# Finishing an encoder layer inside its expert stage: the last stage's tiles handled behind experts 8 to 11, rows rewritten behind 12 to 14

## The reference

```
aff = jax.nn.softmax((xf @ w_router).astype(jnp.float32), axis=-1)
cap = EC_CAPACITY_FACTOR * n // N_EXPERTS          # 2 * 1024 // 16 = 128
gate, idx = lax.top_k(aff.T, cap)                  # each expert picks 128 tokens
xe = xf[idx]
hid = jax.nn.silu(jnp.einsum('ecd,edf->ecf', xe, w_gate)) * jnp.einsum('ecd,edf->ecf', xe, w_up)
ye = jnp.einsum('ecf,efd->ecd', hid, w_down) * gate[..., None].astype(h.dtype)
y = jnp.zeros_like(xf).at[idx.reshape(-1)].add(ye.reshape(-1, D))
...
x = x + gate2 * rmsnorm(expert_choice_moe(h, ...), g_post_ffn)
```

## Time and profile before

| | us |
|---|---|
| median of 3 runs | 2588.22 |
| the profiled execution's own time | 2585.97 |
| its span in the profile | 2584.2 |
| PE busy | 2305.1 (89%) |
| DVE busy | 1200.7 (46%) |
| ACT busy | 1090.8 (42%) |
| POOL busy | 620.2 (24%) |

### The profile page before, as it was taken

How to read it: one execution, slowest core, us unless ns; L and a number is a source line. 1 busy time by engine, 2 the same in 40 slices (tenths; PEclk the granted TensorE clock), 3 DMA queues, 4 the chain that set the end, 5 groups by cost and what they waited for, 6 DMA issues and landing times. The chain is left out here.

```text
span 2584.2 us, 35356 instructions
## 1 busy us (share of the span) xinstructions
PE 2305.1 (89%) x13449; PEld 1920.3 (74%) x13449; DVE 1200.7 (46%) x1847; ACT 1090.8 (42%) x1758; POOL 620.2 (24%) x615
## 2 busy tenths in 40 slices
PE   6999999999999978999606999999999999999940
PEld 4679889678898876677405888888888888888830
DVE  4212344544224346656493555555555545445416
ACT  4213444645434346655312444444444444444412
POOL 2003234233224234534311011111111111101003
PEclk9999999999999989999758999999999999999975
DMA  8635448456454477645345566666666666666529
GB/s 330 229 98 185 141 149 229 128 160 165 149 174 150 155 189 214 202 146 198 108 192 179 201 207 217 219 212 212 215 218 216 215 220 215 203 204 217 180 55 384
DMA packets 234890, 496.09 MB, mean 192 GB/s; under 512 B 36448, under 2 KB 127600, under 8 KB 231696
## 3 DMA queue, kind: packets, MB, share of 16 engines
q1 hardware_dynamic: 196528, 414.31, 47.6%
q0 software_dynamic: 35936, 71.75, 10.5%
q10 hardware_dynamic: 2304, 8.39, 0.8%
HBM read 405.40 MB, written 88.51 MB: 191 GB/s over the span
## 5 line engine op out<-in xcount | busy, mean ns | idle before, releaser
L2252 DVE TENSOR_TENSOR moe_w_lo<-moe_wf,moe_w_hi 128x2048 fp32r<-128x2048 f32 x192 | 439.9, 2292 | 550.7 <-ACT moe_w_hi L2174 550.7
L2174 ACT ACTIVATE moe_w_hi<-moe_wf 128x2048 fp32r<-128x2048 f32 x192 | 367.9, 1916 | 620.6 <-PE moe_acc L2305 602.1
L2305 PE MATMUL moe_acc<-moe_w_hi,moe_x_hi 128*128 128x512 f32 x1024 | 402.6, 393 | 6.9 <-ACT moe_hid L2188 5.5
L2305 PE MATMUL moe_acc<-moe_w_hi,moe_x_lo 128*128 128x512 f32 x1024 | 399.9, 390 | 0.0
L2305 PE MATMUL moe_acc<-moe_w_lo,moe_x_hi 128*128 128x512 f32 x1024 | 399.4, 390 | 0.0
L2305 PEld LDWEIGHTS moe_acc<-moe_w_hi,moe_x_hi 128*128 128x128 f32 x1024 | 192.9, 188 | 46.8 <-issue 6.0
L1732 PE MATMUL banks<-fr_w_hi,fr_h_hi 128*128 128x256 f32 x768 | 225.5, 294 | 0.0
L2305 PEld LDWEIGHTS moe_acc<-moe_w_hi,moe_x_lo 128*128 128x128 f32 x1024 | 192.8, 188 | 40.6
L2305 PEld LDWEIGHTS moe_acc<-moe_w_lo,moe_x_hi 128*128 128x128 f32 x1024 | 193.0, 189 | 39.3
L1732 PE MATMUL banks<-fr_w_lo,fr_h_hi 128*128 128x256 f32 x768 | 218.2, 284 | 0.0
L1732 PE MATMUL banks<-fr_w_hi,fr_h_lo 128*128 128x256 f32 x768 | 218.0, 284 | 0.0
(11 more groups left out here) (257 smaller groups left out, 4198.3 us busy)
## 6 DMA issues: line engine op xcount, KB each, us to landing
moe_wf<-in_w_expert_gate SPq DMA_DIRECT2D x64, 1024.0 KB, 4.9
moe_wf<-in_w_expert_up SPq DMA_DIRECT2D x64, 1024.0 KB, 4.8
moe_wf<-in_w_expert_down SPq DMA_DIRECT2D x64, 1024.0 KB, 5.1
fr_w_raw<-in_w_units SPq DMA_DIRECT2D x28, 1024.0 KB, 6.0
fr_bias<-in_na_bias SPq DMA_DIRECT2D x16, 1520.0 KB, 11.5
fr_a_w<-in_w_ada POOLq DMA_DIRECT2D x16, 1024.0 KB, 6.3
scratch_qk_t<-fr_stage SPq DMA_DIRECT2D x64, 256.0 KB, 2.5
scratch_vov<-fr_stage SPq DMA_DIRECT2D x96, 128.0 KB, 2.0
```

Source lines behind the costliest of these rows:

```text
L2174: nc.scalar.activation(w_hi[:, q, :, :], wf[:, q, :, :], ACT.Copy).then_inc(w_hi_ready, 1)
L2252: nc.vector.tensor_tensor(w_lo[:, q, :, :], wf[:, q, :, :], w_hi[:, q, :, :].bitcast(F32), ALU.subtract).then_inc(w_lo_ready, 1)
L2305: mm = nc.tensor.matmul(acc[:, j, b, :], x[:, g, k, :], w[:, q, a, h * HALF:(h + 1) * HALF], start=(k == 0 and i == 0), stop=(k == KC - 1 ...
```

## The change

`finish` is gone. Its work is cut into 30 units, done by the engines of `experts` in windows of four behind the experts. Units 0 to 15 are the 16 whole tiles, in windows of the bodies of experts 9 to 12, that is, when the adds of experts 8 to 11 have landed. Units 16 to 29 are the 128 rows that one of experts 9 to 15 picked in one group: their y and x1 are gathered again by index, and the result overwrites these rows of `out`. Sixteen to 19 (experts 9 and 10) stand in the body of expert 13, 20 to 23 in 14's, 24 to 27 in 15's. Units 28 and 29 are the rows of expert 15, whose DOWN product is not weighed and scattered any more: DVE adds it from PSUM, times the gate, to the gathered y (`add_last`). Two buffers each, `fy` and `fx`, serve the units in turn. All their DMAs are issued by POOL: `load_unit`, `root`, `store_unit`. ACT has `square`, DVE `mean`, `result`. For experts 8 to 15 the code is written out, the loop covers 0 to 7.

The diff, without declarations and the body of `finish`:

```diff
+    FIRST, UNITS = 8, 4
+    units = [(t // TT, t, None) for t in range(GROUPS * TT)]
+    units += [(g, None, e) for e in range(FIRST + 1, NE) for g in range(GROUPS)]
...
         def over_experts(eng, body):
-            with eng.Fori(0, NE // 2 - 1) as i:
+            with eng.Fori(0, FIRST // 2) as i:
                 for j in range(2):
                     body(i * 2 + j, j)
-            for j in range(2):
-                body(NE - 2 + j, j)
+            for e in range(FIRST, NE):
+                body(e, e % 2)
+        def window(e):
+            return range(UNITS * (e - FIRST - 1), UNITS * (e - FIRST)) if isinstance(e, int) and e > FIRST else range(0)
...
             def body(e, j):
                 load(e, UP)
+                if isinstance(e, int) and e == FIRST:
+                    for g in range(GROUPS):
+                        sp.dma_start(rows[:, g, :], mod_row[g, GATE2:GATE2 + 1, :].to_broadcast([P, D])).then_inc(rows_loaded, 16)
+                    sp.dma_start(fy[:, 0, :], io["g_post_ffn"].to_broadcast([P, D])).then_inc(rows_loaded, 16)
...
+            def load_unit(n):
+                j = n % 2
+                g, t, e = units[n]
+                if n >= 2:
+                    pool.wait_ge(out_stored[j], 16 * (n // 2))
+                if t is not None:
+                    pool.dma_start(fy[:, j, :], y_view[t]).then_inc(fy_loaded[j], 16)
+                    pool.dma_start(fx[:, j, :], x1_view[t]).then_inc(fx_loaded[j], 16)
+                else:
+                    nc.gpsimd.tensor_copy(row_ids[:, j:j + 1], index_c[:, g * NE + e:g * NE + e + 1])
+                    pool.drain()
+                    at = bass.IndirectOffsetOnAxis(ap=row_ids[:, j:j + 1], axis=0)
+                    pool.indirect_dma_start(fy[:, j, :], None, io["y"], at).then_inc(fy_loaded[j], 16)
+                    pool.indirect_dma_start(fx[:, j, :], None, io["x1"], at).then_inc(fx_loaded[j], 16)
+            def root(n):
+                pool.wait_ge(y_mean, n + 1)
+                nc.gpsimd.tensor_tensor(y_r[:, n % 2:n % 2 + 1], y_ss[:, n % 2:n % 2 + 1], mhalf[:, :], ALU.pow).then_inc(y_root, 1)
+            def store_unit(n):
+                j = n % 2
+                g, t, e = units[n]
+                pool.wait_ge(out_ready, n + 1)
+                if t is not None:
+                    pool.dma_start(out_view[t], fx[:, j, :]).then_inc(out_stored[j], 16)
+                else:
+                    pool.wait_ge(out_stored[1 - j], 16 * ((n + 1) // 2))
+                    pool.indirect_dma_start(io["out"], bass.IndirectOffsetOnAxis(ap=row_ids[:, j:j + 1], axis=0), fx[:, j, :], None).then_inc(out_stored[j], 16)
             def body(e, j):
                 if not is_last(e, 2):
                     gather(e + 2, j)
-                scatter(e, j)
+                ns = window(e)
+                if ns:
+                    if ns[0] == 0:
+                        pool.wait_ge(rows_made, 1)
+                    pool.wait_ge(added, (ZEROS + e * GROUPS) * 16)
+                    for half in (ns[0:2], ns[2:4]):
+                        for n in half:
+                            load_unit(n)
+                        for n in half:
+                            root(n)
+                        for n in half:
+                            store_unit(n)
+                if not is_last(e):
+                    scatter(e, j)
             over_experts(pool, body)
-            pool.wait_ge(added, (ZEROS + GROUPS * NE) * 16)
+            nc.gpsimd.tensor_copy(gcol[:, (NE - 1) % 2, :], by_expert(gate_c, NE - 1)).then_inc(gcol_ready, 1)
+            for n in range(LAST, LAST + GROUPS):
+                load_unit(n)
+            for n in range(LAST, LAST + GROUPS):
+                root(n)
+            for n in range(LAST, LAST + GROUPS):
+                store_unit(n)
+            for j in range(2):
+                pool.wait_ge(out_stored[j], 16 * (len(units) // 2))
...
+            def square(n):
+                j = n % 2
+                if n < LAST:
+                    act.wait_ge(fy_loaded[j], 16 * (n // 2 + 1))
+                else:
+                    act.wait_ge(y_whole, n - LAST + 1)
+                act.drain()
+                nc.scalar.activation(zero[:, :], fy[:, j, :], ACT.Square, accum_out=y_ss[:, j:j + 1]).then_inc(y_sq, 1)
...
+                ns = window(e)
                 if is_last(e):
+                    for n in ns[0:2]:
+                        square(n)
                     split(e, DOWN)
                 else:
                     split(e + 1, GATE, range(0, 2))
                     turned_out(e + 1, (x_hi[:, 1 - j], 1 - j), x_turned, x_hi_ready)
+                    for n in ns[0:2]:
+                        square(n)
                     split(e + 1, GATE, range(2, NP))
                     split(e, DOWN, range(0, 2))
+                    for n in ns[2:4]:
+                        square(n)
                 turned_out(e, (h_hi, j), h_turned, h_hi_ready)
                 if not is_last(e):
                     split(e, DOWN, range(2, NP))
                     silu(e + 1, 1 - j)
                     split(e + 1, UP)
-                weigh(e, j)
+                    weigh(e, j)
+                else:
+                    for n in ns[2:4]:
+                        square(n)
             over_experts(act, body)
+            for n in range(LAST, LAST + GROUPS):
+                square(n)
...
+            def mean(n):
+                dve.wait_ge(y_sq, n + 1)
+                nc.vector.tensor_scalar(y_ss[:, n % 2:n % 2 + 1], y_ss[:, n % 2:n % 2 + 1], 1.0 / D, EPS, ALU.mult, ALU.add).then_inc(y_mean, 1)
+            def result(n):
+                j = n % 2
+                dve.wait_ge(y_root, n + 1)
+                nc.vector.scalar_tensor_tensor(fy[:, j, :], fy[:, j, :], y_r[:, j:j + 1], rows[:, units[n][0], :], ALU.mult, ALU.mult)
+                dve.drain()
+                dve.wait_ge(fx_loaded[j], 16 * (n // 2 + 1))
+                nc.vector.tensor_tensor(fx[:, j, :], fx[:, j, :], fy[:, j, :], ALU.add).then_inc(out_ready, 1)
+            def make_rows():
+                dve.wait_ge(rows_loaded, 16 * (GROUPS + 1))
+                for g in range(GROUPS):
+                    a = nc.vector.tensor_tensor(rows[:, g, :], rows[:, g, :], fy[:, 0, :], ALU.mult)
+                a.then_inc(rows_made, 1)
+            def add_last(g, j):
+                n = LAST + g
+                dve.wait_ge(fy_loaded[n % 2], 16 * (n // 2 + 1))
+                for h in range(2):
+                    cut = slice(h * HALF, (h + 1) * HALF)
+                    a = nc.vector.scalar_tensor_tensor(fy[:, n % 2, cut], acc[:, j, 2 * g + h, :], gcol[:, j, g:g + 1], fy[:, n % 2, cut], ALU.mult, ALU.add)
+                a.then_inc(y_whole, 1)
...
+                ns = window(e)
                 if is_last(e):
-                    split(e, DOWN)
+                    for n in ns[0:2]:
+                        mean(n)
+                    split(e, DOWN, range(0, 2))
+                    for n in ns[0:2]:
+                        result(n)
+                    split(e, DOWN, range(2, NP))
                     multiply(e, j)
                 else:
                     split(e + 1, GATE, range(0, 2))
                     turned_out(e + 1, x_hi[:, 1 - j], x_lo[:, 1 - j], 1 - j, x_hi_ready, x_ready)
-                    split(e + 1, GATE, range(2, NP))
+                    for n in ns[0:2]:
+                        mean(n)
+                    split(e + 1, GATE, range(2, 3))
+                    for n in ns[0:2]:
+                        result(n)
+                    split(e + 1, GATE, range(3, NP))
                     multiply(e, j)
                     split(e, DOWN, range(0, 2))
+                    for n in ns[2:4]:
+                        mean(n)
                 turned_out(e, h_hi, h_lo, j, h_hi_ready, h_ready)
+                if is_last(e):
+                    for n in ns[2:4]:
+                        mean(n)
+                for n in ns[2:4]:
+                    result(n)
                 if not is_last(e):
                     split(e, DOWN, range(2, NP))
+                    if isinstance(e, int) and e == FIRST:
+                        make_rows()
                     split(e + 1, UP)
             over_experts(dve, body)
+            dve.wait_ge(piece_done, ONE + piece(NE - 1, DOWN, NP))
+            dve.wait_ge(gcol_ready, ONE + NE)
+            for g in range(GROUPS):
+                add_last(g, (NE - 1) % 2)
+            for n in range(LAST, LAST + GROUPS):
+                mean(n)
+            for n in range(LAST, LAST + GROUPS):
+                result(n)
...
-def finish(nc, io):
...
-    finish(nc, io)
```

More of the change, by code:

```diff
@@ L2025, in experts @@
     BK = 4
+    FIRST, UNITS = 8, 4
+    units = [(t // TT, t, None) for t in range(GROUPS * TT)]
+    units += [(g, None, e) for e in range(FIRST + 1, NE) for g in range(GROUPS)]
+    TILES, LAST = GROUPS * TT, len(units) - GROUPS
+    tok = lambda name: io[name].rearrange("(t p) n -> t p n", p=P)
```

(14 more changed lines are left out.)

88 lines of the change are left out of this document (removed).

## The result

The changed kernel takes **2692.4 us** (median of four runs, 2691.0 to 2693.6), against 2588.5 for the kernel before on the same chip: a ratio of 1.040, 95% interval 1.038 to 1.042, some 104 us slower. The forecast was 2676, in a range of 2637 to 2722.

What follows compares the result with a forecast made beforehand. PE alone was taken to bound the expert stage, with 89 us of idle PE at the end to win. Terms 68.4 + 29.9 + 23.4 - 33.9 = +87.8 on 2586.0 gave 2673.8, as median 2676, range 2637 to 2722.

Steps and rivals of the forecast that it cites:

- The mechanism: Experts 9 to 14: ACT stands at the first square for its tile; splits and multiply queue behind, so PE waits.
- Experts 9 to 12: Windows of whole tiles: multiply ends at +49.7, PE waits 15.5 us, clock adds 1.6; 17.1 per window, +68.4 for four.
- The second half's margin: Second pair of units in windows 9 to 12: h turned out by 59.0, DOWN at 64.0; 5 us spare, no cost.
- Expert 13: Window with gathered rows: each unit's drain waits for all POOL transfers under way, DOWN starts at +76.8 not +46.9, +29.9 us.
- Expert 14: Window with gathered rows like the one before, but no gathers in front, 6.5 less: +23.4 us.
- Expert 15 and the tail: Last body to span end: DOWN ends at 79.9, POOL's chain of stores and gathers ends at 110.9 for 144.8, -33.9 us.
- The sum: Whole kernel: 68.4 + 29.9 + 23.4 - 33.9 = +87.8 us on the profiled 2586.0.
- The rule against the row: POOL transfers: skill page's 3.2 us for 512 KB would give 2641; forecast kept 4.4 per load, 5.4 per store.
- The first (loads hidden): Rival for windows and tail: loads are hidden and the tail is won, 71 us, 2517; chance 0.04.
- The second (drains wait only for scatter-adds): Rival for POOL's drains: windows 13 and 14 cost 17 and 14, tail wins 50; +49, 2637; chance 0.09.
- The third: Rival: second half binds in every window, each issue after the stall paying 1.6 more; +40, 2716; chance 0.16.
- Written-out experts: Experts 8 to 13 written out straight instead of looped: put down at nothing, bodies 68.9 us each.

Runs made afterwards that it cites:

- e2: Changed kernel with its squares, means and results at later places in ACT's and DVE's queues, gate columns copied ahead of the window; 2593.1 us, ratio 1.002.
- e4: Changed kernel keeping the windows' loads and stores but without squares, means, roots and results of units 0 to 27; 2557.7 us, ratio 0.989 to the kernel before.
- e6: Changed kernel without loads and stores of units 0 to 27, their squares and results kept; 2540.8 us, ratio 0.981 to the kernel before.
- e3: Changed kernel with only DVE's two first results moved behind the multiply in experts 9 to 14; 2715.3 us, ratio 1.049 to the kernel before.
- e1: Kernel before with experts 8 to 15 written out and the loop over 0 to 7, no work moved; 2589.1 us, ratio 1.000.
- e8: Changed kernel with row work reordered, one drain per gathered pair, a pair's stores independent, expert 15's two tiles gathered ahead; 2549.2 us, ratio 0.984.

## Why the prediction was right, and where its sizes were off

*The mechanism* is shown. The forecast said that ACT would stand at the first square, with the splits and so multiply behind it; e2 moves the squares and experts 9 to 12 come back to 68.8, and e4 and e6 leave out one side and the 18 us become 0 or 3.

*Experts 9 to 12*: 72.4 for 68.4. Multiply ended at +50.2 for +49.7, PE's wait was 15.9 for 15.5, the turn at the low clock 3.67 for 3.4. From its start on, the low clock cost 2.5 in expert 9 for my 1.6: the turn 1.8, and the products behind the rest, the first of which I had alone. *The second half's margin* of 5 us was 4.0 in expert 9 (h turned out at 2089.7, DOWN at +65.4), so it cost nothing, as said; e3 shows how thin it is: there PE came 5.4 sooner and the second pair 4.8 later, and PE waited 6.0.

*Expert 13*: 39.6 for 29.9, the term that was mis-sized most. Along its own steps: y16 was issued at +32.8 for +31.2, and a load, its neighbour and the drain took 7.3 for 6.5, so store 16 went at +52.6 for +50.1 (2.5). From there to the issue of y18 went 12.2 for 11.8. Then y18 to y19 took 10.1 for 6.5 (3.6): I had let one hop stand for all, although the weight loads that were held up behind the square start again just there. Of the loads in windows 13 and 14 only the two beside weight loads were slow, y18 (7.9) and y22 (7.5, between drains of 6.21 and 7.55 us); no run holds the weight loads back, so the link is read from the rows and not tested. h was turned out at +83.5 for +76.8. And DOWN took 24.9 for 21.9, by the low clock after PE's second idle (3.0), which I had counted for the first wait alone. *Expert 14* repeats this with 31.0 for 23.4. That the clock is the reason of the longer DOWN is read from the windows and from e3, where it comes with each second stop; no run changes the clock alone.

*Expert 15 and the tail*: -38.8 for -33.9. DOWN ended at +79.1 for +79.9, and POOL's chain was shorter than put down: the second store of each pair landed in 4.8, 3.3 and 3.3 us for my 5.4. The timeline of POOL with the two last stores, and the tile view of `out` for the pair before:

```profile
2680.67 1.82 POOL L2214 DMA_INDIRECT out<-moe_fx,moe_parts  x1 [1.18 <-DVE moe_fx L2377]
2685.67 0.97 POOL L2214 DMA_INDIRECT out<-moe_fx,moe_parts  x1 [3.17 <-DMA out<-moe_fx,moe_parts]
...
DMA to landing us min/median/max: 3.3/3.7/4.2
```

*The sum*: the windows cost 21.3 us more than forecast, and 4.9 of that is hidden by a tail that came out shorter. So the 16 us between forecast and result flatter the sizes: that the two errors have opposite signs is luck.

*The rule against the row*: the Trainium skill ("DMA: Bandwidth & Descriptors", "Anatomy of one DMA — SWDGE (gpsimd) path") makes 3.2 us of 512 KB. That estimate agrees with the plain and the late stores here (2.9 to 3.8 us in expert 9's body, 3.3 above) and not with the loads: gathers of rows took 4.2 to 4.4 alone and 7.9 beside weight loads, and the plain loads of expert 9's body 5.1 to 8.1, the first two right behind gathers and the others beside weight loads. My sum by rows stayed 16 short, the one by the page 51.

*The rivals*. The first (loads hidden) is refuted by the 17.98 us ahead of the square. The second (drains wait only for scatter-adds) is refuted by drains of 4.55 and 7.64 behind gathers. The third had the mechanism right and the sizes wrong. The second gather takes 0.97 in the windows, and the direct second halves don't bind; but some issues do stretch, and DVE's and POOL's rows of expert 13 show which:

```profile
2428.37 1.28 DVE L2374 SCALAR_TENSOR_TENSOR moe_fy<-moe_fy,moe_parts,moe_rows 128x1024 f32<-128x1024 f32 x1
...
2433.07 2.48 DVE L2365 TENSOR_TENSOR moe_hid<-moe_hid,moe_acc 128x512 f32<-128x512 f32 x4
...
2464.56 4.49 DVE L2352 TENSOR_TENSOR moe_w_lo<-moe_wf,moe_w_hi 128x2048 fp32r<-128x2048 f32 x2
...
2467.41 2.48 POOL L2214 DMA_INDIRECT out<-moe_fx,moe_parts  x1 [3.16 <-DMA out<-moe_fx,moe_parts]
```

The store at 2428.74 starts inside L2374 and takes 1.82; the one at 2467.41 starts inside a split and takes 2.48. Both of these DVE operations read two tiles in SBUF, and the issues end 0.91 and 0.84 us after them. The store at 2433.71 starts inside multiply, which reads `acc` in PSUM beside `hid`, and takes 0.97, as gathers do while DVE is idle. The 2.58 of the earlier trace rows fits too, and so does every other indirect issue of this trace behind expert 8. The Trainium skill ("SBUF — State Buffer", "SBUF: two separate sides") describes the port that DVE and GpSimd share as a lock, which a DVE operation with two SBUF inputs holds for its whole length. The trace agrees. What made this rival's +40 wrong is that few issues on PE's path start inside such an operation: in a window of rows the first store of each pair pays 0.85, and a second store beside a split 1.5. Written-out experts cost nothing, as assumed (e1).

## What to carry to other kernels

Work that fills an engine's idle time has to stand in its queue where its input is already there. The same row work cost 18 us a body ahead of the weight splits and none behind the turned h, 24 us further down the same body (+14.8 and +38.5), as long as its tile had landed by then; in e8 one hadn't. When it waits, count what it held up as starting at once afterwards, and count the clock for every stop of PE, not for the longest alone; a fix that shortens one wait and leaves a second behind it can lose (e3). A saved tail of 90 us is only worth what the chain of transfers that replaces it leaves: here the order gave back 99 us, and it took one drain and one wait less per pair of units, and a gather issued ahead, to turn it into a gain of 41 us over the kernel before.

## What the runs showed that I had not expected

That a drain on POOL waits for gathers and stores as for scatter-adds was in the forecast, and the idles of 4.55 to 7.64 us show it. What it is worth was not: an index copy with a drain in front of each indirect DMA makes a series of them, one landing each, and taking one of two out gave 24 us. POOL's transfers share the DMA engines with SP's weight loads: a 512 KB gather that lands in 4.4 us took 7.9 while 275 to 370 GB/s were moving. And an indirect issue of 0.97 us takes 1.8 to 2.5 when it starts inside a DVE operation that reads two tiles in SBUF.
